# A hybrid layer on one core: gate tiles ahead of the pool groups, another order of the split products, and an end in three chunks

## The reference

```python
z = rmsnorm(h, g_mix) @ w_in                    # 1024 -> 512 + 512 + 1024 + 1024
u_ssm, u_pool, gate_ssm, gate_pool = split(z)
a_out = S5(u_ssm)                               # complex diagonal scan, 32 groups of 16 channels, 64 states
                                                # y = Re(C h) + d*u, gelu(y), (y @ w_glu_a) * sigmoid(y @ w_glu_b)
p_out = pool(u_pool)                            # 4 groups: trailing mean of 2, 4, 8, 16 frames minus the frame,
                                                # then (128 -> 256) products, times pool_scale
merged = sigmoid(gate_ssm) * a_out + sigmoid(gate_pool) * p_out
h = h + merged @ w_out
n2 = rmsnorm(h, g_ffn)
h = h + (silu(n2 @ w_ffn_gate) * (n2 @ w_ffn_up)) @ w_ffn_down
y = rmsnorm(h, g_final)                         # outputs: y and the new S5 and pool states
```

## Time and profile before

| | before |
|---|---|
| device time, median of 3 runs (lowest, highest) | 1367.76 us (1365.76, 1367.93) |
| profiled execution: time, span, granted clock | 1367.73 us, 1365.8 us, 0.981 |
| busy share: PE, DVE, ACT, POOL | 95%, 49%, 23%, 21% |
| `w_hi` of a slab (ACT), `w_lo` of a slab (POOL), mean | 1.04 us, 2.41 us |
| W copy (ACT), x8 | 0.59 us each |
| other waits of PE: first tiles on `w_hi`; `diag`; `sq_sum` | 8.4, 2.5, 3.9 us |
| spill of a pool tile, 528 KB, issue to landing | 3.9 us |

### The profile page before, as it was taken

How to read it: one execution, slowest core, us unless ns; L and a number is a source line. 1 busy time by engine, 2 the same in 40 slices (tenths; PEclk the granted TensorE clock), 3 DMA queues, 4 the chain that set the end, 5 groups by cost and what they waited for, 6 DMA issues and landing times.

```text
span 1365.8 us, 18937 instructions
## 1 busy us (share of the span) xinstructions
PE 1303.2 (95%) x8204; PEld 1291.7 (95%) x8204; DVE 672.0 (49%) x672; ACT 312.7 (23%) x334; POOL 292.2 (21%) x122
## 2 busy tenths in 40 slices
PE   7794799999999999999999999999999999999996
PEld 7794699999999999999999999999999999999996
DVE  6486389860546633334434343434343434343355
ACT  5500421142432222221111111111111111111124
POOL 2201121230222235522111222222222222221110
PEclk9987899999999999999999999999999999999998
DMA  8273442225413251111111111111111111111103
GB/s 302 81 123 41 76 120 67 83 79 109 129 47 91 81 189 46 47 31 47 47 46 46 46 46 46 46 46 46 46 46 45 38 41 44 46 46 47 47 16 127
DMA packets 121686, 95.41 MB, mean 70 GB/s; under 512 B 9072, under 2 KB 108528, under 8 KB 121648
## 3 DMA queue, kind: packets, MB, share of 16 engines
q1 hardware_dynamic: 120496, 94.80, 24.5%
q10 hardware_dynamic: 1152, 0.06, 0.1%
HBM read 78.47 MB, written 13.10 MB: 67 GB/s over the span
## 4 chain that ended last, share of the span: by engine, by line
PE 85%; DVE 7%; issue 3%; ACT 2%; DMA 1%; SPq 1%; POOL 1%; DVEq 0%; ACTq 0%
PE bank_b L410 40%; PE bank_a L410 40%; DVE f_u L887 1%; DVE hT L887 1%; SPq L310 1%; DVE sc_a L887 1%; PE aux L507 1%; DVE S L887 1%; DMA xs<-in_x_turned 1%; PE bank_a L428 1%; PE aux L461 1%; DMA stage<-in_w_in 0%; ACT w_hi L623 0%; PE aux L527 0%; DVE sc_b L887 0%
## 5 line engine op out<-in xcount | busy, mean ns | idle before, releaser
L851 POOL TENSOR_TENSOR w_lo<-stage,w_hi 128x1024 fp32r<-128x1024 f32 x110 | 264.5, 2405 | 998.9 <-ACT w_hi L623 987.6
L623 ACT ACTIVATE w_hi<-stage 128x1024 fp32r<-128x1024 f32 x108 | 111.8, 1035 | 795.3 <-PE bank_b L410 487.4
L410 PE MATMUL bank_b<-hg_hi,w_hi 128*128 128x352 f32 x528 | 113.3, 323 | 0.0
L410 PE MATMUL bank_a<-hg_hi,w_hi 128*128 128x352 f32 x528 | 113.1, 323 | 0.0
L410 PE MATMUL bank_a<-hg_lo,w_hi 128*128 128x352 f32 x528 | 113.1, 322 | 0.0
L410 PE MATMUL bank_a<-hg_hi,w_lo 128*128 128x352 f32 x528 | 113.1, 322 | 0.0
L410 PE MATMUL bank_b<-hg_lo,w_hi 128*128 128x352 f32 x528 | 113.1, 322 | 0.0
L410 PE MATMUL bank_b<-hg_hi,w_lo 128*128 128x352 f32 x528 | 113.1, 322 | 0.0
L887 DVE TENSOR_TENSOR hT<-bank_a,hT 128x1056 f32<-128x1056 f32 x48 | 60.3, 1255 | 79.8 <-PE bank_a L410 79.8
L887 DVE TENSOR_TENSOR hT<-bank_b,hT 128x1056 f32<-128x1056 f32 x48 | 60.3, 1257 | 75.8 <-PE bank_b L410 75.8
L887 DVE TENSOR_TENSOR f_u<-bank_b,rstd_row 128x1056 f32<-128x1056 f32 x22 | 27.7, 1258 | 140.3 <-PE bank_b L410 140.3
(11 more groups left out here) (248 smaller groups left out, 2312.9 us busy)
## 6 DMA issues: line engine op xcount, KB each, us to landing
stage<-in_w_in SPq DMA_DIRECT2D x22, 512.0 KB, 4.4
stage<-in_w_ffn_gate SPq DMA_DIRECT2D x22, 512.0 KB, 3.6
stage<-in_w_ffn_up SPq DMA_DIRECT2D x22, 512.0 KB, 3.6
stage<-in_w_ffn_down SPq DMA_DIRECT2D x22, 512.0 KB, 3.7
xs<-in_x_turned SPq DMA_DIRECT2D x8, 528.0 KB, 7.9
mp_scratch<-gate_t SPq DMA_DIRECT2D x8, 528.0 KB, 3.9
pool_t<-mp_scratch SPq DMA_DIRECT2D x8, 528.0 KB, 3.7
hT<-in_x_turned SPq DMA_DIRECT2D x8, 528.0 KB, 7.0
```

What stands on the lines that cost most here:

```text
L410: mm = pe.matmul(banks[:, b, 0:BLK], w[:, slot, col:col + P], x[:, k, b * BLK:(b + 1) * BLK], start=(i == 0 and step == 0), stop=(i == len ...
L623: act.activation(w_hi[:, slot, 0:cols], stage[:, slot, 0:cols], ACT.Copy).then_inc(hi_ready, 1)
L851: pool.tensor_tensor(w_lo[:, slot, 0:cols], stage[:, slot, 0:cols], w_hi[:, slot, 0:cols], ALU.subtract).then_inc(lo_ready, 1)
```

## The change

- `S_GATE`/`T_GATE` come before `S_POOL`/`T_POOL`. TensorE's order is now: tiles 0 to 3, `rstd_rows(1)`, gate tiles 0 to 7 with `turn_k` after gate 1, `turn_w` after gate 2 and `turn_v` after gate 3 (which now holds the wait for all W copies), pool groups 0 and 1, `turn_y`, pool groups 2 and 3, GLU.
- Gates are evacuated into `gate0`, `gate1`, `gate_s`, take their sigmoid there, are spilled to `gate_scratch` by SP and loaded again in the GLU (`sig_s`).
- The 16 DMAs into `TO` are issued by ScalarE, after gate 1's sigmoid and before the split of slab 4 and the W copies. The fill of `TO` waits for the spill of gate 0, the W copies for the spill of gate 1.
- ScalarE loads its function table with a Copy at the start; the Sin of the constants comes earlier.
- VectorE: inverse_root after the constants; the scaling of u in the middle of the CA operations; the scan beside gate tiles 4 to 7; `scan_fill` in group 0; gelu 0 and 1 in group 2, gelu 2 and 3 in group 3. ScalarE stacks S and takes Y at the end of group 1.
- `tile()`: bank outside, step inside: the three products of one bank follow each other.
- End: the last two pairs of hidden blocks in 24 tiles of 12 matmuls over token chunks of 384, 384 and 288 columns; squares of five channel blocks added by POOL, the sum over them and the other two by three products with an all-ones matrix per chunk; rstd per chunk on VectorE over all partitions; h scaled there, and 24 output DMAs, channel-major (the host transposes y).

```diff
-S_POOL, T_POOL = 4, 4
-S_GATE, T_GATE = 20, 24
+S_GATE, T_GATE = 4, 4
+S_POOL, T_POOL = 12, 12
+T_LAST = T_TAIL + 4
+CHUNKS = ((0, 384), (384, 384), (768, 288))
...
 SP
+            for n in range(4):
+                gate_slab(n)
             sp.wait_ge(u_scaled, KS)
             sp.dma_start(u_dram..., UT[:, :, :, :]).then_inc(ut_out, 16)
             sp.wait_ge(ut_out, 16)
             for i in range(L):
                 sp.dma_start(U[16 * i:16 * i + 16, :, :], ...).then_inc(u_in, 16)
+            spill_gate(0)
+            gate_slab(4)
+            spill_gate(1)
+            gate_slab(5)
...
+                sp.dma_start(sig_s[:, r, :], gate_dram[n * P:(n + 1) * P, :]).then_inc(gate_in[r], 16)
                 sp.dma_start(pool_t[:, r, :], mp_dram[n * P:(n + 1) * P, :]).then_inc(mp_in[r], 16)
...
 TensorE, tile()
-                    for step, (w, x) in enumerate(((w_hi, hi), (w_hi, lo), (w_lo, hi))):
-                        for b in range(3):
+                    for b in range(3):
+                        for step, (w, x) in enumerate(((w_hi, hi), (w_hi, lo), (w_lo, hi))):
...
+            for n in range(KD):
+                pe.wait_ge(lo_ready, S_GATE + 1 + n)
+                if n == 1:
+                    pe.wait_ge(row_used, 1)
+                tile(T_GATE + n, bank_b if n % 2 else bank_a, n % 2, ALL, x_hi, x_lo)
+                if n == 1:
+                    turn_k()
+                if n == 2:
+                    turn_w()
+                if n == 3:
+                    turn_v()
+            for g in range(4):
                 pool_group(g)
+                if g == 1:
+                    turn_y()
...
+            def chunk_squares(b):
+                c0, c = CHUNKS[b]
+                pe.wait_ge(sq_used, sq_adds(b + 1))
+                pe.matmul(aux[:, b % 2, 0:c], ones[:, :], sq_sum[:, c0:c0 + c], start=True, stop=False)
+                for n in (6, 7):
+                    pe.wait_ge(sq_ready, KD * (b + 1) + n + 1)
+                    mm = pe.matmul(aux[:, b % 2, 0:c], ones[:, :], sq_slot(KD * b + n), start=False, stop=(n == 7))
+                mm.then_inc(ss_turned, 1)
...
+            for i in range(3 * KD):
+                if i >= 6:
+                    pe.wait_ge(evac_done, T_LAST + i - 5)
+                    last_down(i, 0)
+                if i in (0, 4):
+                    pe.wait_ge(lo_ready, S_TAIL + 7 + i // 4)
+                last_down(i, 1).then_inc(tile_done, 1)
+                if i >= KD and i % KD == 0:
+                    chunk_squares(i // KD - 1)
+            chunk_squares(2)
...
 ScalarE
+            gate(1)
+            act.wait_ge(k_ready, 1)
+            act.wait_ge(to_zero, 1)
+            for i in range(L):
+                j = L - 1 - i
+                for g2 in range(2):
+                    act.dma_start(TO[16 * i:16 * i + 16, g2:G:2, 16 * j:P],
+                                  K_sb[16 * g2:16 * g2 + 16, :, 0:P - 16 * j]).then_inc(to_in, 16)
+            split_gate(4)
+            act.wait_ge(gate_out[1], 16)
+            take_w()
...
 POOL
             pool.wait_ge(wt_ready, 1)
+            pool.wait_ge(gate_out[0], 16)
             pool.memset(TO[:, :, :], 0.0).then_inc(to_zero, 1)
...
 VectorE
+            for g in range(4):
+                take_pool(g)
+                if g == 0:
+                    scan_fill(0)
+                if g == 3:
+                    gelu(2)
+                pool_gate(g, 0)
+                if g >= 2:
+                    gelu(0 if g == 2 else 3)
+                pool_gate(g, 1)
+                for r in range(2):
+                    pool_last(g, r)
+                if g == 0:
+                    scan_fill(1)
+                if g == 2:
+                    gelu(1)
...
+            def chunk_rstd(b):
+                c0, c = CHUNKS[b]
+                mean, root, tmp, row = f_g[:, 0:c], f_s[:, 0:c], f_u[:, 0:c], rstd_row[:, c0:c0 + c]
+                dve.wait_ge(ss_turned, 2 + b)
+                dve.tensor_scalar(mean, aux[:, b % 2, 0:c], 1.0 / D, EPS, MUL, ADD).then_inc(ms_ready, 1)
+                dve.wait_ge(root_ready, 3 + b)
+                then(dve.reciprocal(row, root))
+                then(dve.scalar_tensor_tensor(tmp, row, -0.5, row, MUL, MUL))
+                then(tt_(tmp, tmp, mean, MUL))
+                then(dve.scalar_tensor_tensor(row, tmp, 1.5, row, ADD, MUL))
+
+            for i in range(3 * KD):
+                n, b = i % KD, i // KD
+                add_last(i)
+                if b and n == 1:
+                    chunk_rstd(b - 1)
+                if b and 3 <= n:
+                    for m in ((0, 1), (2, 3), (4, 5), (6,), (7,))[n - 3]:
+                        scale_last(KD * (b - 1) + m)
+            chunk_rstd(2)
             for n in range(KD):
+                scale_last(2 * KD + n)
```

More of the change, by code:

```diff
@@ L345, in _ @@
[L345 to L350, removed]
+            for q in gate_out:
+                sp.wait_ge(q, 16 * 4)
             for n in range(KD):
                 r = n % 2
-                half = slab3(r)
-                slab(S_GLU + n, r, [(half[:, 0:4], w_a[:, :, n * P:(n + 1) * P]),
-                                    (half[:, 4:8], w_b[:, :, n * P:(n + 1) * P])])
@@ L385, in _ @@
                     slab(S_TAIL + 4 + 2 * i + r, r, [(down[r], w_d[:, f:f + 2, r * 4 * P:(r + 1) * 4 * P])])
[L386 to L391, removed]
+            for i in range(3 * KD):
+                n, (c0, c) = i % KD, CHUNKS[i // KD]
+                sp.wait_ge(y_scaled, i + 1)
+                sp.dma_start(t_out["y"][n * P:(n + 1) * P, c0:c0 + c], chunk(hT, i)).then_inc(y_stored, 16)
+            sp.wait_ge(y_stored, 16 * 3 * KD)
             sp.wait_ge(small_out, 16)
@@ L497, in pool_group @@
                 tile(t0 + 4, odd, 1, [(P, 0)], hi, lo)
[L499 to L509, removed]
@@ L531, in _, with turn_v @@
-            with pe.Fori(1, 4) as m:
-                for r, banks in enumerate((bank_a, bank_b)):
-                    pe.wait_ge(lo_ready, 2 * m + (S_GATE + 1 + r))
-                    tile(2 * m + (T_GATE + r), banks, r, ALL, x_hi, x_lo)
+            def turn_v():
+                pe.wait_ge(u_in, 16 * L)
+                pe.wait_ge(w_evac, 8)
+                for pr in range(PAIRS):
+                    if pr >= 2:
+                        pe.wait_ge(v_evac, pr - 1)
+                    for comp in range(2):
+                        for g2 in range(2):
+                            mm = pe.matmul(aux[64 * g2:64 * g2 + 64, (pr + 1) % 2, comp * NCG:(comp + 1) * NCG],
+                                           W[:, comp, pr, 64 * g2:64 * g2 + 64], U[:, 2 * pr + g2, :], start=True, stop=True)
+                    mm.then_inc(v_turn, 1)
@@ new lines, in turn_y @@
+            def turn_y():
+                pe.wait_ge(v_evac, PAIRS)
+                pe.wait_ge(s_stacked, 4)
+                pe.wait_ge(ca_stacked, 64)
+                pe.wait_ge(to_in, 32 * L)
+                for r in range(12):
+                    g2, prs = r % 2, range(3 * (r // 2), min(3 * (r // 2) + 3, PAIRS))
+                    if r >= 2:
+                        pe.wait_ge(y_evac, r - 1)
+                    for i, pr in enumerate(prs):
+                        out = aux[:, g2, i * NCG:(i + 1) * NCG]
+                        pe.matmul(out, TO[:, 2 * pr + g2, :], U[:, 2 * pr + g2, :], start=True, stop=False)
+                        mm = pe.matmul(out, CA_st[:, 2 * pr + g2, :], S_st[:, 2 * pr + g2, :], start=False, stop=True)
+                    mm.then_inc(y_turn, 1)
@@ L616, in _, with split @@
+            chunk_squares(2)
         @block.scalar
         def _(act):
-            def split(s, slot, landed, done, cols=SLAB):
+            def split(s, slot, landed, done, cols=SLAB, to=w_hi):
                 act.wait_ge(stage_in[slot], landed)
@@ L622, in split @@
                     act.wait_ge(tile_done, done)
[L623 removed]
+                act.activation(to[:, slot, 0:cols], stage[:, slot, 0:cols], ACT.Copy).then_inc(hi_ready, 1)
             def landed(s):
@@ L671, in _ @@
             square(2)
+            square(3)
             split(3, 1, landed(3), 2)
             raw_u(1)
-            for tt in range(3, TT):
+            act.wait_ge(angle_ready, 1)
+            act.activation(pt[:, 8:10, :], pt[:, 6:8, :], ACT.Sin).then_inc(sine_ready, 1)
+            for tt in range(4, TT):
                 square(tt)
@@ L730, in gate @@
-            def gate(n):
-                split(S_GATE + n + 2, n % 2, landed(S_GATE + n + 2), T_GATE + n + 1)
-                act.wait_ge(evac_done, T_GATE + n + 1)
-                g_at = gate_at(n)
-                act.activation(g_at, g_at, ACT.Sigmoid).then_inc(gs_sig, 1)
-            for comp in range(2):
-                act.wait_ge(s_ready, comp + 1)
-                for g2 in range(2):
-                    act.activation(S_st[64 * comp:64 * comp + 64, g2:G:2, :], S[64 * g2:64 * g2 + 64, comp, :, 0:NCG],
-                                   ACT.Copy).then_inc(s_stacked, 1)
```

(63 more changed lines are left out.)

507 lines of the change are left out of this document (251 added, 256 removed).

## The result

Eleven runs of the changed kernel have a median of 1369.31 us (1367.24 to 1372.02), eleven of the kernel before 1366.46 us. The ratio is 1.002, with a 95% interval from 1.0012 to 1.0029: slower by a margin that is small but clear, where 1362 us had been forecast. The profiled execution is the changed kernel's fastest, 1367.24 us with a span of 1365.4, at a granted clock of 0.984 where the median of the eleven is 0.981. So the profile shows 5.2 us of what the forecast lacks; the median is another 2.1 us above it, in runs of which there is no trace.

What follows compares the result with a forecast made beforehand. TensorE was taken as full in the middle, where only a matmul's price counts; start and end could gain by order of work. 1367.73 - 0.5 - 1.8 - 3.5 = 1361.9, forecast 1362 us, own range 1356 to 1367, overall 1348 to 1372.

Steps and rivals of the forecast that it cites:

- Middle: 0.: GLU's first matmul to the end of the last gate/up tile: swapped loops change nothing, 72 matmuls still take 11.52 us.
- rival D: Tile matmuls: order of banks matters; fast 1298 us (chance 0.04), or slower, 5 ns a matmul making 1398 (chance 0.05).
- Start: Up to the end of V: 150.9 us, where it was 161.6 before.
- The W wait: TensorE between gate tiles 2 and 3 idles 18.4 us for gate 0's spill, TO's fill, 16 issues and the first W copy.
- rival B: Wait for W shrinks by 10: ScalarE issues at 0.45 us, gate 0's spill doesn't wait for U's end; 1352 us, chance 0.18.
- V to the GLU: From V's end to the GLU's start: 208.3 us of work plus 26.6 of waits, ending at 385.8, 1.8 us earlier.
- Y's wait: Ahead of Y, after group 1: 9.1 us for ScalarE's stacking of S after split 5, then 2.6 of half clock.
- the wait of the last product: Group 3: last pool products wait 9.2 us because two gelus stand ahead of two evacuations; then 2.6 of half clock.
- the small waits: V to the GLU: some 1.7 us for a bank in group 0, and two group changes at 0.8 each for weights.
- C: Pool groups: VectorE, a queue in order, becomes late and holds TensorE's banks; 1371 us, or 1374; chance 0.17.
- End: After the last gate/up tile: 67.5 us to the span's end instead of 71.0, 3.5 us earlier.
- E: Whole kernel: start and end gain, new waits give all of it back; 1366 to 1368 us, chance 0.06.

Runs made afterwards that it cites:

- two moves of a few lines: Changed kernel, old loop order: ScalarE's 16 TO issues behind the W copies, 1354.29 us; or its stacking of S ahead of group 1's last two weight splits, 1354.23 us.
- the best kernel: Changed kernel with the old loop order, TO issues behind the W copies and stacking of S ahead of two weight splits: 1343.49 us, ratio 0.9809.

## Why the prediction was wrong

**The step that failed is "Middle: 0."** I took 0 for the swapped loops because each matmul has its own weight load and the only row with 16 passes into one bank was slow "by its type". No row of before showed the order, and I said so; but I then gave the slow side of rival D 0.05 of the chance, though its price (1.2 ns a matmul undoes the forecast) was so small that nothing in the profile could exclude it. Measured, it is 1.1 ns, in most but not all of the tiles: 3.8 us of the middle and 0.8 ahead of it in the profiled execution. The same step had no term for half clock in the middle, and 1.5 us of it came, behind products that the change does not touch. Together they are the 5.2 us by which the middle grew, and that is all that the profiled execution (1367.24) lacks to 1362. The bounds of this step were left to rival D, which the range of the forecast leaves out.

**The other steps, against the profile after.**

- Start. V's last products end at 150.1 us, 150.9 had been forecast; u's write is issued at 76.3 (75.6). The W wait is 18.5 (18.4), with the causes in the order given, as the chain of the changed kernel shows (the landing of gate 0's spill, the fill, the first issue, the first copy):

```profile
93.44 13.00 DMA gate_scratch<-gate
106.55 3.52 POOL TO L942
110.14 0.75 ACTq L763
...
121.90 0.59 ACT W L770
```

- ScalarE's issue: 16 in 10.69 us, 0.67 each, so the value with the same pattern (0.66, from SP) was right and 0.45 wrong. The Trainium skill's sentence that an issue is "usually small relative to the DMA itself" ("DMA: Bandwidth & Descriptors", section "Issuing engines are not separate DMA queues") would have led to rival B. Taken one by one the trace agrees with it: 0.67 us of issue, 2.0 to 5.8 us from issue to landing. But sixteen in a row made 10.7 us ahead of copies on the critical path, and moving them behind those copies gave 10 us.
- V to the GLU. Y's wait 9.1 (9.1), the wait of the last product 8.0 (9.2), each followed by half clock (0.50 in the windows 283 to 286 and 382.3 to 385.3); the GLU starts at 385.3 (385.8). That it agrees to half a microsecond is luck in part. Y was put at 12.5 us, from 305.81 on the earlier trace rows, but in the timeline of before Y starts ahead of that row:

```profile
302.79 0.39 PE L527 MATMUL aux<-U,TO 128*128 128x133 f32 x2
```

  Y took 15.5 us there and 17.1 in the changed kernel (282.46 to 299.53), some 2 of them for half clock. What this adds, and the 0.8 of slow tiles, is made up by terms that were too large: the last wait, the half clock behind it (nine matmuls took 3.0 us, those at 270.24 had taken 1.45, so 1.6 and not 2.6) and the small waits (1.2 us, put at 3.3). C, VectorE late by 8.6 us, did not come.
- End. 67.6 us behind the last gate/up tile (67.5), through the chain that was named. Two misses cancel in it: the last add ended 55.5 us behind that tile (54.7), the last transfer took 2.8 us and not 4. Its last steps on VectorE, reciprocal, three operations, eight scalings:

```profile
1355.60 1.95 DVE L1422 RECIPROCAL rstd_row<-f_s 128x288 f32<-128x288 f32 x1 [0.51 <-ACT f_s L914]
1357.59 0.46 DVE L1423 SCALAR_TENSOR_TENSOR f_u<-rstd_row 128x288 f32<-128x288 f32 x1
...
1359.06 3.52 DVE L1431 SCALAR_TENSOR_TENSOR hT<-hT,gains,rstd_row 128x288 f32<-128x288 f32 x8
```

  The reciprocal was put at 1.6 and took 1.95 us, the scalings at 3.4 and 3.52; at 1349.71 nine elements had taken 0.21.

- Sums. The 0.5 us of the first wait is taken off twice, in the 57.1 from which 385.8 follows and again in the last line: the sum's own terms give 1362.4. The waits ahead of the GLU add to 26.8, not 26.6. For V the terms named lead from 139.8 to 149.7; the 1.2 up to 150.9 is the evacuation of gate 3, which is not named (1.27 us from 139.24 in the trace). And by the program the 16 records of rstd's product are eight matmuls in two banks, so that row says little of a bank that is kept.

So the waits and chains of two of the three stages were right, their lengths to within a microsecond in part by luck, and one edit that was put at 0 cost some 5 us, which with the half clock took back what they gained. E (the gains given back by new waits) was not it; rival D was, on its slow side, though not by the mechanism it names: six in a row in one bank ran at 11.52.

## What to carry to other kernels

An edit inside the innermost loop is multiplied by the number of matmuls: 1.1 ns on most of 7272 of them cost some 5 us, more than the 2.9 that the rest of the change gained by medians, so such an edit is timed alone and never sent along with another. Where no row shows an order, its chance of going either way is not small because its price per instruction is. A wait whose releaser is a queue in order can be attacked by moving what stands ahead on that queue: two moves of a few lines were worth 10 us each here.

## What the runs showed of the hardware that was not expected

- Two paces of the same matmul at full clock, 160.0 and 161.1 ns for 352 columns, without a value between; the second only where each bank was kept for exactly three matmuls, not for one, for two and one, or for six. The cause is open.
- A fall to half clock with no idle time ahead of it: behind the nine one-column products of the sum of squares (18 records, 1.93 us) TensorE ran at 0.50 for some 3 us in the changed kernel, with the old loop order (0.53 in its window) and in the best kernel (the half tile again 7.51 us), but at 1.00 before, with the same instructions; of the profiled executions of the twelve kernels six had the long half tile (7.51 or 7.53 us), six 5.96, that of before among them. What tips it was not tried.
